# Latent products last in the turn of the first expert loop, and the context's up products in the bank of the turned hidden values

## The reference

```python
aff = softmax(h @ router_w)                  # 16 experts
g, idx = top_k(swapaxes(aff, 1, 2), cap)     # cap = 128 latent tokens, 32 context tokens per expert
xe = hf[flat].reshape(b, 16, cap, 1024)
a = einsum('becd,edf->becf', xe, w_gate)     # f = 1408
u = einsum('becd,edf->becf', xe, w_up)
y = einsum('becf,efd->becd', silu(a) * u, w_down)
out = zeros.at[flat].add(y * g)              # back to the tokens' rows, then a residual add
```

## Time and profile before

| | us |
|---|---|
| median of 3 runs | 3567.95 (3567.95 to 3575.17) |
| the profiled execution, its own time | 3570.9 |
| its span, first to last instruction | 3569.0 |
| of it the mixed expert stage, first context product to last latent product | 885 to 2048 |
| mean granted clock of TensorE over the span | 0.921 |

### The profile page before, as it was taken

How to read it: one execution, slowest core, us unless ns; L and a number is a source line. 1 busy time by engine, 2 the same in 40 slices (tenths; PEclk the granted TensorE clock), 3 DMA queues, 4 the chain that set the end, 5 groups by cost and what they waited for, 6 DMA issues and landing times. The chain is left out here.

```text
span 3569.0 us, 61226 instructions
## 1 busy us (share of the span) xinstructions
PE 3032.9 (85%) x24750; PEld 2475.3 (69%) x24750; DVE 2068.5 (58%) x2213; ACT 1790.0 (50%) x2016; POOL 479.2 (13%) x250
## 2 busy tenths in 40 slices
PE   6599787976999999999999939992957999999993
PEld 2488643543787788877878737661436999999993
DVE  0522374344666666666666644554256888888884
ACT  2411153333555555555545445765235777777773
POOL 1111142002010101011010003332020000000000
PEclk8699899987999999999999959996978999999997
DMA  7211100237777777777777531101236999999995
GB/s 317 73 36 42 48 1 25 100 118 315 264 257 249 265 250 257 260 251 250 270 249 257 198 96 36 30 24 45 105 149 234 357 354 358 386 362 357 357 361 176
DMA packets 137950, 726.17 MB, mean 203 GB/s; under 512 B 10709, under 2 KB 13525, under 8 KB 109829
## 3 DMA queue, kind: packets, MB, share of 16 engines
q1 hardware_dynamic: 125064, 684.99, 51.0%
q0 software_dynamic: 12288, 37.75, 4.6%
q10 hardware_dynamic: 384, 0.24, 0.0%
HBM read 680.90 MB, written 42.04 MB: 203 GB/s over the span
## 5 line engine op out<-in xcount | busy, mean ns | idle before, releaser
L1543 DVE TENSOR_TENSOR mixed_low<-mixed_raw,mixed_high 128x3072 fp32r<-128x3072 f32 (+1 forms) x192 | 592.8, 3094 | 393.7 <-ACT mixed_high L1477 390.8
L1477 ACT CAST mixed_high<-mixed_raw 128x3072 fp32r<-128x3072 f32 (+1 forms) x192 | 489.3, 2552 | 492.1 <-DMA mixed_raw<-in_moe 479.0
L1964 DVE TENSOR_TENSOR rows_low<-rows_raw,rows_high 128x2816 fp32r<-128x2816 f32 x188 | 581.3, 3093 | 79.4 <-ACT rows_high L1908 70.2
L1908 ACT CAST rows_high<-rows_raw 128x2816 fp32r<-128x2816 f32 x188 | 479.4, 2559 | 115.1 <-PE ps L1815 66.6
L1399 PE MATMUL ps<-mixed_high,mixed_xhi 128*128 128x384 f32 (+1 forms) x1024 | 345.9, 338 | 0.5 <-DVE mixed_low L1543 0.5
L1813 PE MATMUL ps<-rows_high,rows_xhi 128*128 128x352 f32 x1024 | 337.5, 330 | 6.0 <-issue 4.5
L1400 PE MATMUL ps<-mixed_low,mixed_xhi 128*128 128x384 f32 (+1 forms) x1024 | 331.4, 324 | 0.0
L1401 PE MATMUL ps<-mixed_high,mixed_xlo 128*128 128x384 f32 (+1 forms) x1024 | 331.2, 323 | 0.0
L1815 PE MATMUL ps<-rows_high,rows_xlo 128*128 128x352 f32 x1024 | 329.9, 322 | 0.0
L1814 PE MATMUL ps<-rows_low,rows_xhi 128*128 128x352 f32 x1024 | 329.6, 322 | 0.0
L1387 PE MATMUL ps<-mixed_raw,mixed_xc 128*32 128x96 f32 (+1 forms) x8192 | 197.9, 248 | 69.6 <-issue 31.5
(11 more groups left out here) (286 smaller groups left out, 5861.2 us busy)
## 6 DMA issues: line engine op xcount, KB each, us to landing
rows_raw<-in_moe_rows SPq DMA_DIRECT2D x192, 1408.0 KB, 8.0
mixed_raw<-in_moe SPq DMA_DIRECT2D x144, 1536.0 KB, 6.4
ring_r<-in_ada_w SPq DMA_DIRECT2D x24, 2048.0 KB, 17.4
mixed_raw<-in_moe SPq DMA_DIRECT2D x48, 1024.0 KB, 6.7
w_raw_r<-in_ev_in SPq DMA_DIRECT2D x18, 512.0 KB, 3.5
w_raw_u<-in_od_in SPq DMA_DIRECT2D x16, 512.0 KB, 3.6
x_res<-ring_r SPq DMA_DIRECT2D x10, 512.0 KB, 2.6
x_norm<-ring_r SPq DMA_DIRECT2D x10, 512.0 KB, 2.9
```

The lines of the kernel that those rows point to most:

```text
L1477: act.copy(r.high[:, p % SLOTS, 0:nj, :], r.raw[:, p % SLOTS, 0:nj, :]).then_inc(high_done, 1)
L1543: dve.tensor_tensor(r.low[:, p % SLOTS, 0:nj, :], r.raw[:, p % SLOTS, 0:nj, :], r.high[:, p % SLOTS, 0:nj, :].bitcast(F32), ALU.subtract). ...
L1908: act.copy(high[:, p % SLOTS, :], raw[:, p % SLOTS, :]).then_inc(high_done, 1)
L1964: dve.tensor_tensor(low[:, p % SLOTS, :], raw[:, p % SLOTS, :], high[:, p % SLOTS, :].bitcast(F32), ALU.subtract).then_inc(low_done, 1)
```

## The change

- The context's up products go to bank 4, where the turned latent hidden values lie, and not to bank 6. They now wait for `hT_low` of the group before (`split_h` of group u - 1; for group 0, of the last group of the expert before) and no longer for `sac_done`.
- The context's gate products wait for `sac_done` of the group before, no longer for `hc_done`.
- `turn_h` waits for `hc_done` of its own group, no longer for `hT_low`.
- `turn_h` of the last group moves from the end of its turn to the next turn, behind the first context products and ahead of the first latent products. A turn on TensorE so ends with latent products.
- ScalarE's silu is in two functions. At place 0 the silu of the context comes before `copy_h`, then comes the silu of the latent products. At places 3, 6 and 9 `copy_h` comes first, as it did.
- VectorE reads the context's up products in bank 4; its order of work is as before, as are those of SyncE and GpSimd.

```diff
@@ context (TensorE)
                 if kind == 0:
-                    need(pe, hc_done, owner * 4 + u)
+                    need(pe, sac_done, owner * 4 + u)
                 elif kind == 1:
-                    pe.wait_ge(sac_done, owner * 4 + (u + 1))
+                    need(pe, hT_low, owner * 4 + u)
...
-                            out = m.ps[32 * g:32 * g + 32, 6, P * kind:P * kind + 32 * nj].rearrange("p (j n) -> p j n", j=nj)
+                            out = m.ps[32 * g:32 * g + 32, 6 - 2 * kind, 0:32 * nj].rearrange("p (j n) -> p j n", j=nj)
@@ turn_h (TensorE)
                 pe.wait_ge(h_done, e * 4 + (u + 1))
-                need(pe, hT_low, e * 4 + u)
+                pe.wait_ge(hc_done, e * 4 + (u + 1))
@@ turn (TensorE)
                     if exists(e, p):
                         context(e, b, p)
+                    if p == 0 and later(e):
+                        turn_h(e - 1, 3)
+                    if exists(e, p):
                         latent(e, b, p)
-                    if p in (2, 5, 8, 11) and expert(e):
+                    if p in (2, 5, 8) and expert(e):
                         turn_h(e, p // 3)
@@ silu, turn (ScalarE)
-            def silu(e, p):
+            def silu_context(e, p):
                 u = group_of[p][1]
                 n = len(GJ[u])
                 act.wait_ge(ctx_done, number(e, p))
                 need(act, hc_done, e * 4 + (u - 1))
                 act.activation(r.sac[:, u % 2, 0:32 * n], m.ps[:, 6, 0:32 * n], ACT.Silu).then_inc(sac_done, 1)
+
+            def silu(e, p):
...
             def turn(e, b):
                 for p in range(TURN):
+                    if p in (3, 6, 9) and expert(e):
+                        copy_h(e, p // 3 - 1)
+                    if p in GATE_AT and expert(e):
+                        silu_context(e, p)
                     if p == 0 and later(e):
                         copy_h(e - 1, 3)
-                    if p in (3, 6, 9) and expert(e):
-                        copy_h(e, p // 3 - 1)
                     if p in GATE_AT and expert(e):
                         silu(e, p)
@@ multiply (VectorE)
-                dve.tensor_tensor(r.hc[:, u % 2, 0:32 * n], m.ps[:, 6, P:P + 32 * n], r.sac[:, u % 2, 0:32 * n],
+                dve.tensor_tensor(r.hc[:, u % 2, 0:32 * n], m.ps[:, 4, 0:32 * n], r.sac[:, u % 2, 0:32 * n],
```

More of the change, by code:

```diff
@@ L1499, in silu @@
                 act.activation(r.sac[:, u % 2, 0:32 * n], m.ps[:, 6, 0:32 * n], ACT.Silu).then_inc(sac_done, 1)
+            def silu(e, p):
+                u = group_of[p][1]
+                n = len(GJ[u])
                 act.wait_ge(piece_done, number(e, p))
```

## The result

| | before | after |
|---|---|---|
| median of runs, us | 3567.95 (3567.43 to 3575.17, 4 runs) | 3747.94 (3743.11 to 3749.56, 4 runs) |
| ratio to before | | 1.0497, 95% interval 1.0479 to 1.0515 |
| span of the profiled execution, us | 3569.0 | 3744.7 |
| mean granted clock | 0.921 | 0.898 |

The change makes the kernel 180 us slower. The page of the changed kernel shows TensorE 65 us busier for the same 24750 products. The second row is the mixed expert stage, in the columns of rows 2: it now lasts from 888 to 2226.

The account below looks back on a forecast made before the run. TensorE was taken to bound the changed stage. Later starts of 113 us plus 70 for the clock, less about 13, gave 170 us on 3570.9, so 3741, and 3738 for the median; range 3668 to 3805.

Parts of the forecast that it names:

- The new wait: Up products at places 1, 4, 7 and 10 wait for the late `split_h`; starts 113 us later in sum.
- place 4: Up products here start 3.7 us later in 15 turns, with turn 0 put at 1; together 57 us.
- Place 1: Up products after a turn's end or jump back: change of 0, between -8 and +21 us over 15 turns.
- place 10: Up products here start 3.4 us later in 15 turns, nothing in the last turn; together 51 us.
- Place 7: Up products here: 35 us as it stood, but the chain shortens as a transfer avoids GpSimd's additions; 5 us taken.
- The jump: TensorE's gap at the jump back goes, about 4 us in 7 places, but is worth nothing behind place 1's wait.
- The clock: TensorE runs at half speed after the new stalls: 40 falls of 1.75 us, 70 us, ends 38 and 127.
- A fall: One drop of TensorE's clock after a stall, slowing the products behind it: 1.75 us, between 1.26 and 2.3.
- The sum: Later starts of 113 us and slow products of 70 make 183; about 13 taken off, hence 170 us slower.
- The deduction: About 13 us taken off for chains that shorten with fewer transfers in flight and a lower clock ahead.

Follow-up runs that it names:

- the transposes alone: The kernel before with only the last group's transposes moved behind the next turn's first context products, up products staying in bank 6: 3539.65 us, ratio 0.9933.
- the bank alone: The changed kernel with TensorE's order of before, so up products in bank 4 but a turn still ending with the last group's transposes: 3742.3 us, ratio 1.0494.
- the one with fillers: The changed kernel with 22, 28 and 30 unread products issued ahead of the up products at places 1, 4 and 10: 3712.96 us, ratio 1.0431.
- the early silu: The kernel before with the transposes moved, bank 6 kept, and ScalarE's context silu ahead of the rounding of the piece four places on: 3536.25 us, ratio 0.9922.
- the fastest kernel: The kernel before with moved transposes, bank 6 kept, context's silu ahead of the rounding, and VectorE's `copy_xc` at place 9, not 10: 3520.56 us, ratio 0.987.

## Why the prediction was right

*The new wait.* It was read from rows that already existed, and its distances held. From the down piece's context products to the up products I put 13.6, 13.84, 10.83 and 13.31 us at places 1, 4, 7 and 10. Means over the turns are 13.7, 13.75, 10.8 and 13.4. That VectorE's order, with the split ahead of `split_h`, makes the chain longer than TensorE's work is shown by the run which moves `split_h` alone: the loss of 180 us disappears, with the landing at place 4 where it was. In the prediction's own terms, the up products start later by 55 us at place 4, 52 at place 10 and nothing at places 1 and 7, summed over the turns: 107, where I had put 57, 51, 0 and 5, or 113. (The waits themselves grew by 118.5, because other waits and slow products ahead of these starts went away.)

Place 1 came out right by two slips that cancel. I counted seven jumps, and there are six; and I took turn 7's 15.92 us for all of them, where their mean in the kernel before is 16.7. With six at 15.92 my mean would have been 13.35 in place of 13.6; the trace's is 13.7.

*Place 7.* The 5 us, near turn 0's chain of 9.97, were right in kind: in turn 6 the chain is 1438.24 - 1428.25 = 9.99 us and no turn waits. The reason given is borne out by the trace: GpSimd's additions begin before place 4's stall is over (1418.73), and place 8's transfer, issued when place 4's context products end (1421.52), comes after them:

```profile
1414.60 1.61 POOL L1351 DMA_INDIRECT x_res<-mixed_ys,idx  x1 [39.94 <-DVEq L1614]
1416.51 3.04 POOL L1353 DMA_INDIRECT x_res<-mixed_ysc,idxc  x1 [0.30 <-issue]
...
1428.11 2.77 ACT L1480 CAST mixed_high<-mixed_raw 128x3072 fp32r<-128x3072 f32 x1 [4.87 <-DMA mixed_raw<-in_moe]
```

ScalarE begins to round place 8's piece 6.6 us after those context products here, and 10.1 us after them in turn 6 of the kernel before; in its turn 0, without additions, it is 6.7. The DMA packets of turn 6 show the same: in the first 4 us after place 4's context products, the additions moved 0.5 MB and the weights 0.2 MB before, and 0.02 and 0.8 MB after. No run was made for it alone.

*The jump.* Its gap went altogether, in six places and not seven, and it was worth nothing here. Both halves are shown, by the transposes alone (24 to 29 us gained) and by the bank alone (the same time with or without them). The expected gain of 28 us without the bank lies within the interval of the ratio (17 to 31).

*The clock.* A fall cost (22.1 + 29.3 + 27.9) / 45 = 1.76 us, taken between the changed kernel and the one with fillers, where I took 1.75. That it agrees to 0.01 is luck, for 1.75 was a choice between 1.26 and 2.3. Against the kernel before, the time behind the late starts grew by less, 67 us or 1.5 for each fall, because pauses within the small products of places 4 and 10 went away at the same time. The number of falls was off: 45 of the 46 stalls ended in slow products, where I had 40, because place 1 falls in 15 turns of 15 and not in 10. I had inferred from 3.06 us without a fall that its 2.8 us would mostly be too short. Its stalls turned out at 3.34 us on average, and even one of 2.87 was followed by slow products. They are longer than I put them because TensorE is free after 10.35 us and not 10.7: the 10.7 held a wait of 0.30 us for `copy_xc` ahead of place 0, which went.

*The sum.* 113 + 70 less 13 for chains that might shorten, hence 170. Measured in the same terms it is 107 + 67, which is 174 us of the stage. The deduction had no row behind it, and its reason did not come true: the chains came out at the lengths I had taken (13.55 us for 13.5 at place 1, 13.6 for 13.74 at place 4). It brought the sum near because the two terms were each a little too large, and that is luck too. Without it the forecast is 3751, with it 3738; the measured 3747.94 lies between.

*What I said the profile would show*: 45 waits with 170 us (46 with 180.9), a stage of 1163 + 170 (1338), a clock of 0.92 to 0.94 (0.91), a DMA share of 0.65 (0.67), under 2 us at the jumps (none). The Trainium skill's rule in "TensorE: Matmul & The Clock Gate", "What's actually happening", that activity releases the throttle, agrees with the runs as far as they go: with the stalls filled, the clock was 0.99 for 0.91.

## What to carry to other kernels

Before a wait on one semaphore is exchanged for a wait on another, look up in the trace when the new one is reached today, in every place of the turn. Here, in turn 6, it came 2.3 to 3.6 us after the point where it would be needed, and the reason stood in the order of an engine that the change did not touch. A stall that recurs in a loop can cost more than its own length: here 1.76 us of slow products came on top of each 4 us, while with `split_h` moved, its waits of 1.15 us on average left the clock up at place 4 (1.53 us for 64 products, in all turns but one). And a wait that shows in the profile can be taken away where it is made: the silu was late because ScalarE did it behind a rounding, and moving it needed no other bank. But a wait that is taken away can come back under another name: that move alone gained nothing clear of the noise, and only with `copy_xc` moved too did the time fall, to 0.987.

## What the runs showed of the hardware

- The length of an idle time alone did not decide whether TensorE's clock fell. After 3.06 us idle the products ran at full speed in the kernel before; after 2.87 us in the changed kernel they were slow (granted clock 0.68), as after all 45 stalls between 2.87 and 5.09 us. Only behind the 46th, of 0.82 us, the products ran at full speed. The other runs spread further: at place 0, the granted clock was 1.00 after 3.45 us idle with the early silu, and 0.77 after 1.94 us with the bank alone.
- Long products are not always a low clock. Pauses for issue of about 0.4 us lay within runs of 64 small products: in the kernel before 4.4 us at place 10, and 15.6 us at places 4 and 10 in the fastest kernel, whose granted clock in the stage was 1.00. There 64 products took 2.80 us for 1.10. Their cause is open.
- TensorE's gap at a jump back was 3.4 to 4.9 us in the kernel before and 1.9 to 2.3 us with the bank alone, which both end a turn with transposes. In the kernels that end it with latent products, it was between nothing and 2.6 us. So what stands last is not all that sets it.
